# Keys and values multiplied ahead of the second convolution half, attention's background work begun earlier, in a two-block transformer kernel on one Trainium2 core

## The reference, cut to what matters

```
u = rms_norm(h, norm_mix[i])
q, k, v, c, g = jnp.split(u @ w_in[i], splits, axis=-1)   # 512, 128, 128, 1024, 2048 columns
q = rms_norm(q.reshape(B, S, 8, 64), q_norm[i])
k = rms_norm(k.reshape(B, S, 2, 64), k_norm[i])
y_attn = window_attention(q, k, v, sink[i], rel_bias) @ w_attn_out[i]
c_val, c_gate = jnp.split(c, 2, axis=-1)
c = c_val * jax.nn.sigmoid(c_gate)
c = depthwise_conv(c, conv_w[i], conv_b[i])               # 31 taps, 512 channels
c = jax.nn.silu(layer_norm(c, conv_ln_g[i], conv_ln_b[i]))
y_conv = c @ w_conv_out[i]
g_attn, g_conv = jnp.split(jax.nn.sigmoid(g), 2, axis=-1)
h = h + (g_attn * y_attn + g_conv * y_conv) @ w_o[i]
```

## Time and profile before

| | us |
|---|---|
| median of 3 runs (lowest, highest) | 1773.43 (1772.69, 1773.87) |
| the profiled execution, its own time | 1772.86 |
| its span in the profile | 1771.1 |
| TensorE busy | 1753.6 (99% of the span) |
| VectorE busy | 1165.8 (66%) |
| ScalarE busy | 934.2 (53%) |

### The profile page before, as it was taken

How to read it: one execution, slowest core, us unless ns; L and a number is a source line. 1 busy time by engine, 2 the same in 40 slices (tenths; PEclk the granted TensorE clock), 3 DMA queues, 4 the chain that set the end, 5 groups by cost and what they waited for, 6 DMA issues and landing times.

```text
span 1771.1 us, 26218 instructions
## 1 busy us (share of the span) xinstructions
PE 1753.6 (99%) x9886; PEld 1531.2 (86%) x9886; DVE 1165.8 (66%) x1716; ACT 934.2 (53%) x1380; POOL 26.5 (1%) x32
## 2 busy tenths in 40 slices
PE   9999999999999999999999999999999999999998
PEld 8888888898888988898889888889898888989886
DVE  6665588766655666468876664668574746857473
ACT  6554456645544555455655553567453536745352
POOL 0000000000000000000000000000000000000000
PEclk9999999999999999999999999999999999999999
DMA  8755523544555554542454545544355543435551
GB/s 310 218 190 173 208 95 144 189 174 173 190 184 190 191 190 178 202 167 96 146 187 173 191 178 190 178 139 145 111 197 195 186 163 119 146 111 197 195 185 48
DMA packets 45842, 303.04 MB, mean 171 GB/s; under 512 B 5104, under 2 KB 6256, under 8 KB 12312
## 3 DMA queue, kind: packets, MB, share of 16 engines
q1 hardware_dynamic: 45720, 301.36, 48.0%
HBM read 300.02 MB, written 1.31 MB: 170 GB/s over the span
## 4 chain that ended last, share of the span: by engine, by line
PE 93%; DVE 4%; ACT 2%; issue 1%; POOLq 0%; POOL 0%; ACTq 0%; DVEq 0%
PE psG L500 13%; PE psG L502 12%; PE psG L501 12%; PE psG L578 9%; PE psP L578 5%; PE psSO L578 5%; PE psG L584 5%; PE psG L551 3%; PE psG L552 3%; PE psG L553 3%; PE psSO L584 3%; PE psP L584 3%; PE psP L617 1%; DVE acc L1789 1%; PE psP L881 1%; PE psSO L905 1%
## 5 line engine op out<-in xcount | busy, mean ns | idle before, releaser
L1609 DVE TENSOR_TENSOR wlo<-raw,whi 128x1024 fp32r<-128x1024 f32 (+4 forms) x388 | 655.9, 1703 | 310.9 <-ACT whi L1085 310.7
L1085 ACT ACTIVATE whi<-raw 128x1024 fp32r<-128x1024 f32 (+4 forms) x388 | 554.0, 1443 | 275.1 <-PE psG L502 162.2
L500 PE MATMUL psG<-whi,x 128*128 128x512 f32 (+3 forms) x544 | 207.8, 382 | 0.0
L502 PE MATMUL psG<-whi,x 128*128 128x512 f32 (+3 forms) x544 | 200.9, 369 | 0.0
L501 PE MATMUL psG<-wlo,x 128*128 128x512 f32 (+3 forms) x544 | 200.5, 369 | 0.0
L500 PE MATMUL psG<-whi,hid_hi 128*128 128x512 f32 x472 | 184.1, 390 | 0.0
L502 PE MATMUL psG<-whi,hid_lo 128*128 128x512 f32 x472 | 183.7, 389 | 0.0
L501 PE MATMUL psG<-wlo,hid_hi 128*128 128x512 f32 x472 | 183.6, 389 | 0.0
L578 PE MATMUL psG<-x,whi 128*128 128x512 f32 x704 | 179.8, 392 | 0.0
L551 PE MATMUL psG<-x,wlo 128*128 128x256 f32 x512 | 147.5, 288 | 1.4 <-DVE wlo L1609 1.4
L578 PEld LDWEIGHTS psG<-x,whi 128*128 128x128 f32 x704 | 126.6, 189 | 22.6
(11 more groups left out here) (388 smaller groups left out, 2793.1 us busy)
## 6 DMA issues: line engine op xcount, KB each, us to landing
raw<-in_w SPq DMA_DIRECT2D x261, 1024.0 KB, 4.8
raw<-in_w SPq DMA_DIRECT2D x12, 768.0 KB, 4.2
raw<-in_w SPq DMA_DIRECT2D x14, 512.0 KB, 3.3
raw<-in_w SPq DMA_DIRECT2D x4, 576.0 KB, 3.5
raw<-in_w SPq DMA_DIRECT2D x4, 432.0 KB, 3.2
bias<-line_scratch SPq DMA_DIRECT2D x8, 192.0 KB, 10.9
h<-in_x SPq DMA_DIRECT2D x2, 512.0 KB, 5.4
out<-h SPq DMA_DIRECT2D x2, 512.0 KB, 2.7
```

The lines of the kernel that those rows point to most:

```text
L500: e.matmul(o, ph, wh, start=first, stop=False)
L502: i = e.matmul(o, pl, wh, start=False, stop=last)
L1085: e.activation(w_at(whi, j, off, n), raw[:, j % RAW, off:off + n], ACT.Copy).then_inc(s_hi, count)
L1609: e.tensor_tensor(w_at(wlo, j, off, n), raw[:, j % RAW, off:off + n], f32(w_at(whi, j, off, n)), ALU.subtract).then_inc(s_lo, count)
```

## The change

Four things are done, in each of the two first mixers:

1. The piece `kv_` stands ahead of `c1[0]` and `c1[1]` in the weights' order and in the code of all three engines; the PSUM banks of the two are exchanged with it.
2. The attention generator enters `bg` behind `kv_` as before, which is now ahead of `c1`, and has fewer empty steps: the queries are transposed in its first step instead of its second, the keys in its second instead of its sixth, and the first head's scores stand in its fourth instead of its seventh.
3. In the gates, ScalarE's loop ticks ahead of each half that it prepares; before, `use` prepared a half first.
4. VectorE's code follows: it normalises the queries and keys ahead of `c1`, and its `gated(1)` comes behind `c1`, which is now later.

```
                 out += crossed(c0, halves("w_in", l, (0, 512)))
-                out += c1 + [piece("w_in", l, LO + HI, (512, 768))]
+                out += [piece("w_in", l, LO + HI, (512, 768))] + c1
...
             def attention1(l):                      # TensorE
-                yield
                 for n in range(2):
                     b = spare(("qT", l, n))
...
-                for _ in range(4):
-                    yield
+                yield
                 b = spare(("kT", l))
...
                 spare_frees(b, (s_kl, 4 * l + 4))
+                yield
                 yield
...
-                columns_(c1[0], bank("mix", l, 2), "mix", l)
-                columns_(c1[1], bank("mix", l, 2), "mix", l)
-                free[bank("mix", l, 2)] = [[(s_cvl, 2 * l + 2)]] * 2
+                simple(kv_, X, need, bank("mix", l, 2), True, True)
+                free[bank("mix", l, 2)] = [[(s_kv, 2 * l + t + 1)] for t in range(2)]
                 bg.append(att)
-                simple(kv_, X, need, bank("mix", l, 3), True, True)
-                free[bank("mix", l, 3)] = [[(s_kv, 2 * l + t + 1)] for t in range(2)]
+                columns_(c1[0], bank("mix", l, 3), "mix", l)
+                columns_(c1[1], bank("mix", l, 3), "mix", l)
+                free[bank("mix", l, 3)] = [[(s_cvl, 2 * l + 2)]] * 2
...
+                use(kv_, end=False)                 # ScalarE
+                for t in range(2):
+                    e.wait_ge(s_used, NUM[kv_] + 1)
+                    e.activation(kv[:, t, :], BANKS[bank("mix", l, 2)][t][:, 0:256], ACT.Copy, scale=rsq(n, 4 + t)).then_inc(s_kv, 1)
+                tick()
+                bg.append(att)
                 use(c1[0])
                 use(c1[1], end=False)
                 sigmoid_of(1)
                 tick()
...
                 for g in range(4):
                     u = halves("w_in", l, (1792 + 512 * g, 2304 + 512 * g))
-                    use(u[0])
-                    use(u[1])
+                    for p in u:
+
+                        tick()
+                        high(NUM[p] + AHEAD, True)
+                        tick()
+                        high(NUM[p] + AHEAD)
...
-                use(c1[0])                          # VectorE
+                low(NUM[kv_] + AHEAD, True)
+                tick(2)
                 for t in range(2):
...
                     e.tensor_tensor(o, i0, i1, ALU.mult).then_inc(s_qn, 1)
-                use(c1[1])
-                gated(1, c1[1])
-                bg.insert(0, att)
-                use(kv_, end=False)
+                low(NUM[kv_] + AHEAD)
+                tick()
...
                     e.tensor_tensor(kk, kk, i1, ALU.mult).then_inc(s_kn, 1)
+                bg.insert(0, att)
+                use(c1[0])
+                use(c1[1])
+                gated(1, c1[1])
```

More of the change, by code:

```diff
@@ L1306, in mixer1 @@
                 tick()
-                bg.append(att)
-                use(kv_, end=False)
[L1309 to L1312, removed]
                 for g in range(4):
                     u = halves("w_in", l, (1792 + 512 * g, 2304 + 512 * g))
-                    use(u[0])
-                    use(u[1])
+                    for p in u:
[3 more added lines that the diff above has]
+                        high(NUM[p] + AHEAD)
                     for t in range(2):
@@ L1859, in attention1 @@
                                                op0=ALU.mult, op1=ALU.subtract).then_inc(s_ql, 1)
-                for _ in range(3):
-                    yield
+                yield
                 _, b = TBU["kT", l]
@@ L1912, in gated @@
                     gt, vl = tmp[:, u * 1024:u * 1024 + 512], tmp[:, u * 1024 + 512:u * 1024 + 1024]
-                    ps = BANKS[bank("mix", l, 2 * u)]
+                    ps = BANKS[bank("mix", l, 3 * u)]
                     e.wait_ge(s_used, NUM[spec] + 1)
```

## The result

| | us |
|---|---|
| before, median of 4 runs | 1773.49 (1772.69 to 1773.87) |
| changed, median of 4 runs | 1788.92 (1788.56 to 1790.22) |
| ratio, 95% interval | 1.0089 (1.0071 to 1.0106) |
| profiled execution of the changed kernel: its time, its span | 1789.18, 1787.3 |

The change makes the kernel 15.4 us slower, 0.9%. The forecast was 1784.3 us (10.9 slower). Its own range ended at 1788, and the widest one that was given at 1789.0. The median lies above the first and at the very edge of the second; the measured ratio applied to the earlier median of 1773.43 gives 1789.2, just outside.

A forecast was written before the change was run, and what follows sets the result against it. TensorE, busy 1753.6 of 1771.1 us, was taken as the bound, so only its pauses count: +9.4 us gave 1782.8, plus 1.5 for the clock 1784.3 us. Own range 1780.5 to 1788, over all cases 1778.5 to 1789.

The forecast's parts named there:

- What goes: TensorE's pauses before the keys' transposes and the first product with values vanish in each first mixer: 2.3 us a layer.
- the keys' wait: TensorE's old pause before the keys' transposes, 1.33 us a layer, forecast to go.
- the values' wait: TensorE's old pause before the first product with values, 0.97 us a layer, forecast to go through ScalarE's tick-first loop.
- The scores' wait: TensorE's pause before the first scores, waiting for VectorE's low parts of the keys: 3.6 us a layer, replacing 1.47.
- The tail: TensorE's new pause before the channels' transposes, waiting for VectorE's last multiply-adds of the convolution: 4.9 us a layer.
- Sum without the clock: Pauses gone and added: -3.8 + 3.6 + 4.9 = +4.7 us a layer, +9.4 in the program, giving 1782.8 us.
- the three pauses: TensorE's old pauses before keys' transposes, first scores and first product with values: 3.8 us a layer, 7.5 in the program.
- The clock: TensorE's clock may halve behind the two new 4.9 us pauses: 0 to 5 us, taken as 1.5 for both.
- the two long pauses: The new 4.9 us pauses before the channels' transposes, one in each layer, where the forecast let the clock fall.
- The clock falls in both long pauses and in the scores' pause too: Rival: three clock falls in TensorE's new pauses at 1.7 to 2.5 us each, about 1788 to 1790 us; chance 0.06.

The follow-up runs named there:

- e7: e4 with ScalarE's loop in the gates as before (a half prepared first, then the tick): 1764.75 us, 0.9955 of the kernel before.
- e8: The kernel before with only ScalarE's loop in the gates changed to tick first: 1774.33 us, 1.0012 of the kernel before.
- e3: The changed kernel with one ScalarE `whi` rounding step moved ahead of its first attention step: 1778.10 us, 1.0029 of the kernel before.
- e2: The changed kernel with five instead of four of VectorE's last 62 multiply-adds in a tick: 1775.86 us, 1.0010 of the kernel before.
- e5: The changed kernel with attention's empty steps put back, so only keys and values are moved ahead: 1786.32 us, 1.0078 of the kernel before.
- e1: The changed kernel with useless matmuls filling TensorE's pauses before the first scores (14) and the channels' transposes (20): 1781.00 us, 1.0045 of the kernel before.
- e4: The changed kernel with the edits of e2 and e3 together: 1764.64 us, 0.9952 of the kernel before.
- e6: e5 with five instead of four of VectorE's last multiply-adds in a tick: 1775.16 us, 1.0013 of the kernel before.

## Why the prediction was right or wrong

- *What goes.* Right in sum: the keys' wait and the values' wait are gone. The reason given for the second was wrong. It was not ScalarE's loop that ticks first (e7: no difference; e8: worse), but attention's earlier start, which takes the copy out from behind the tanh.
- *The scores' wait.* Right. Forecast 3.6 us, measured 3.59 by starts, through the very steps: VectorE's idle 5 us measured 5.02, the keys' low parts 255.8 measured 255.9. e3 confirms the cause.
- *The tail.* Right. Forecast 4.9, measured 4.87; T + 16.7 against T + 16.64. e2 and e5 confirm that it is the later start of the 62 multiply-adds.
- *Sum without the clock.* Forecast 1782.8; e1, the changed kernel with the clock kept up, has 1781.0. By the table of starts most of the 1.8 us can be placed. From L695 to the transposes, e4, with no pause, is 4.09 us below before, where the three pauses were put at 3.77; and e1 is at 98.93, where 90.60 + 8.46 makes 99.06. That is 0.45 in a layer, 0.9 in the program. Another 0.5 lies ahead of the mixer (L695 at 220.43 in e1, 220.94 before), and 0.3 is the median of before in that round (1773.16 against 1773.43).
- *The clock.* Here the forecast failed. The step that failed is the term "I take 1.5 for both together". It measured 7.6 us (e1 against the changed kernel, each beside before), 7.3 by starts. Two things were wrong. The clock was given a chance to fall only in the two long pauses, and it fell behind the two of 3.4 us as well (the tail of the kernel before had shown only that it had fallen by 4 us after TensorE's last record, not when). And for each fall the price was taken at a fraction of the 2.5 us of the program's start, on the ground that the pause hides the first part of a slow stretch. It hid 0.6 and 0.8 us in layer 0 and nothing in layer 1; a fall cost 1.9 us on average.
- *The rival that came true.* "The clock falls in both long pauses and in the scores' pause too" is what happened, and its 1788 to 1790 holds the result. It was given 0.06. Its price for a fall, 1.7 to 2.5, was right; its count of three was not, as the scores' pause comes in both layers and makes four. There is luck in both. The sum without the clock was 1.8 too high, which hid part of the miss (6.4 us without that, 4.6 with it), and on the measured 1781.0 this rival's three falls would have come to 1788.5 at most, below the result.

The Trainium skill ("TensorE: Matmul & The Clock Gate", "Part 1: The HAM clock gate") says that the clock is halved after idling, and that the watching runs free of the kernel. e1 agrees with the first: with the pauses filled the mean clock is 0.999. The second fits the runs of e2, with mean clocks of 0.999 and of 0.996 to 0.997 for the same code. In the changed kernel itself it shows little: the prediction let executions scatter by up to 5 us, and the four runs lie within 1.7.

## What to carry to other kernels

When TensorE is 98% busy, work out each remaining pause by following the in-order queues of the engines that feed it: hand sums from start to start gave each new pause within 0.1 us here, while the sum over a layer was off by 0.45. Pauses of 3.4 to 4.7 us cost their length and then 1.3 to 2.8 us more in clock each, so count every pause of that length, in every layer, not just the longest. When attention or any other generator is pulled ahead, look at what it pushes back: here `c1`'s 62 multiply-adds, which a fifth multiply-add in a tick brings in again, and one rounding step that had slipped behind a wait. With both mended the order of the change is worth 8.5 us (e4, 0.5% faster than before). The fifth multiply-add was not tried in the kernel before.

## What the runs showed of the hardware

- The granted clock fell behind pauses of 3.4 us in both layers of the profiled execution of the changed kernel. In e8 it fell too, with no pause longer than 1.6 us; rows of e8 in the second layer, the pause before the product with values and the stretches behind it:

```profile
842.50 0.77 PE L732 MATMUL psSO<-kv,qn 128*128 128x64 f32 x5 [1.57 <-ACT qn L1225]
```

```profile
843.00:844.00 1.00, 1.00 (x10) 1.00 (x10) 1.00 (x4) 1.00 (x6) 0.00 (x0) 0.77 0.54 123
844.00:846.00 2.00, 2.00 (x9) 1.81 (x9) 1.29 (x2) 1.48 (x3) 0.00 (x0) 0.50 1.04 442
```

  The same pause in its first layer had no slow stretch, and the kernel before, with pauses of 0.8 to 1.3 us in the same places, had none in its profiled execution. e5 has the same on the other side: a slow stretch behind its pause of 1.5 us in layer 0 (granted clock 0.50 from 275 to 277) and none behind that of 1.5 us in layer 1. e6 has one behind a pause of 1.8 us in layer 1 (0.50 from 831 to 834) and none behind those of 1.8 and 2.0 us in layer 0. So in these runs the clock fell behind some pauses of under 2 us and not behind others of the same length. The kernel before may know this too: 7 of its 54 runs beside the experiments have a mean clock of 0.998 and took 1773.6 to 1774.2 us, the others 1772.0 to 1773.4; no profile of such a run was taken.
- The program's first 24 records of 128 columns took 5.49 us in the changed kernel, 5.12 in e1 and 4.27 in e8, though their code is the same. So starts inside the program can be compared only from a common point, as in the table of starts.
- Matmuls that compute nothing of use are worth their issue in a pause: 68 of them made the changed kernel 7.6 us faster, each kernel measured against before in its own round.
